# A hybrid encoder trunk on one core: the order of the branch weights' loads and of their split

## The reference, cut to what matters

```python
merged = None
for i, y_i in enumerate((ya, yb, yc)):
    z = cols(COL_Z + i * BRANCH_WIDTH, BRANCH_WIDTH)
    g = cols(COL_G + i * D_MODEL, D_MODEL)
    u = jax.nn.sigmoid(g) * ((y_i * jax.nn.silu(z)) @ w_br[i])
    merged = u if merged is None else merged + u
out = merged @ w_out
return x + gate[:, None, :] * out
```

## Time and profile before

| what | value |
|---|---|
| median of 3 runs | 2371.23 us (2370.74 to 2372.26) |
| time of the profiled execution | 2368.96 us |
| its span on the core | 2366.0 us |
| TensorE matmuls busy | 2309.8 us, 98% of the span |
| VectorE busy | 1624.0 us, 69% |
| ScalarE busy | 1123.7 us, 47% |
| DMA engines busy, all of SP's requests | 20.0% of 16 engines |
| granted TensorE clock, mean | 0.999 |

### The profile page before, as it was taken

The page is one execution under the profiler, slowest core; times in us unless marked ns, Lnnn a source line. Parts: engine busy times, 40 slices in busy tenths (PEclk is TensorE's granted clock), DMA queues, the critical chain, the costliest instruction groups (busy, mean ns, idle before and its releaser), DMA issues.

```text
span 2366.0 us, 41870 instructions
## 1 busy us (share of the span) xinstructions
PE 2309.8 (98%) x15466; PEld 2139.8 (90%) x15466; DVE 1624.0 (69%) x4481; ACT 1123.7 (47%) x3035; POOL 59.0 (2%) x103
## 2 busy tenths in 40 slices
PE   7999999999999999999999999999999999999999
PEld 5888888999999899999888889989999997999998
DVE  7877568577777575666578866775787765666772
ACT  5666457434444443334356674663444435333340
POOL 0010011000000000000001001100000000000000
PEclk9999999999999999999999999999999999999999
DMA  7221321121111322221521112112111122222223
GB/s 279 94 75 37 115 85 43 64 83 57 59 54 45 114 73 67 94 85 63 171 81 35 36 47 96 42 50 98 52 61 35 57 82 81 85 85 76 85 84 122
DMA packets 63034, 186.11 MB, mean 79 GB/s; under 512 B 9584, under 2 KB 22512, under 8 KB 59888
## 3 DMA queue, kind: packets, MB, share of 16 engines
q1 hardware_dynamic: 52320, 164.00, 20.0%
q10 hardware_dynamic: 10512, 19.44, 2.3%
HBM read 168.73 MB, written 12.58 MB: 77 GB/s over the span
## 4 chain that ended last, share of the span: by engine, by line
PE 85%; DVE 6%; ACT 4%; DMA 2%; issue 2%; SPq 0%; ACTq 0%; DVEq 0%
PE ps_proj L984 57%; PE ps_score L1028 7%; PE ps_pt L1028 6%; PE ps_score L1161 2%; PE ps_pt L1174 2%; PE ps_pv L1210 2%; PE ps_score L1145 1%; DMA wb_raw<-in_w_branch 1%; PE ps_tr L1225 1%; PE ps_pv L1191 1%; PE ps_tr L1226 1%; PE ps_pv L1204 1%; DMA w_raw<-in_w 1%; DVE w_lo L2311 1%; ACT act_hi L1435 1%
## 5 line engine op out<-in xcount | busy, mean ns | idle before, releaser
L984 PE MATMUL ps_proj<-w_hi,act_hi 128*128 128x384 f32 x1824 | 632.6, 347 | 3.3 <-ACT act_hi L1435 2.1
L984 PE MATMUL ps_proj<-w_hi,act_lo 128*128 128x384 f32 x1824 | 612.2, 336 | 0.0
L984 PE MATMUL ps_proj<-w_lo,act_hi 128*128 128x384 f32 x1824 | 611.8, 335 | 0.0
L984 PEld LDWEIGHTS ps_proj<-w_hi,act_hi 128*128 128x128 f32 x1824 | 342.8, 188 | 9.1 <-ACT act_hi L1435 5.8
L984 PEld LDWEIGHTS ps_proj<-w_lo,act_hi 128*128 128x128 f32 x1824 | 343.4, 188 | 0.0
L984 PEld LDWEIGHTS ps_proj<-w_hi,act_lo 128*128 128x128 f32 x1824 | 342.5, 188 | 0.0
L1954 DVE TENSOR_REDUCE ssq<-square 128x2 f32<-128x256 f32 (+1 forms) x228 | 95.6, 419 | 215.5 <-ACT square L1529 214.7
L1529 ACT ACTIVATE square<-ps_proj 128x256 f32<-128x256 f32 x228 | 88.2, 387 | 270.7 <-PE ps_proj L984 270.1
L2311 DVE TENSOR_TENSOR w_lo<-w_raw,w_hi 128x1536 fp32r<-128x1536 f32 (+3 forms) x121 | 188.7, 1560 | 12.6 <-ACT w_hi L1359 12.0
L1359 ACT ACTIVATE w_hi<-w_raw 128x1536 fp32r<-128x1536 f32 (+2 forms) x120 | 161.1, 1343 | 56.5 <-DMA w_raw<-in_w 33.0
L984 PE MATMUL ps_proj<-act_hi,w_hi 128*128 128x512 f32 (+1 forms) x512 | 174.4, 341 | 8.2 <-DVE w_lo L2311 4.8
(11 more groups left out here) (263 smaller groups left out, 4895.0 us busy)
## 6 DMA issues: line engine op xcount, KB each, us to landing
w_raw<-in_w SPq DMA_DIRECT2D x80, 768.0 KB, 5.2
w_raw<-in_w SPq DMA_DIRECT2D x40, 512.0 KB, 3.7
s_raw<-in_w_gate SPq DMA_DIRECT2D x72, 256.0 KB, 3.0
w_ada<-in_w_mod SPq DMA_DIRECT2D x11, 1536.0 KB, 6.7
wb_raw<-in_w_branch SPq DMA_DIRECT2D x24, 512.0 KB, 3.7
first_ada<-in_w_first SPq DMA_DIRECT2D x8, 1024.0 KB, 13.2
parked<-y_t ACTq DMA_DIRECT2D x4, 1536.0 KB, 7.1
w<-in_w_gate SPq DMA_DIRECT2D x24, 256.0 KB, 4.0
```

The lines of the kernel that those rows point to most:

```text
L984: op = pe.matmul(out, sta[s](k), mov[m](k), start=(k == 0 and n == 0), stop=(k == chunks - 1 and n == 2))
```

## The change

It has two parts.

In `load_groups`, the branch weights of group `g + 1` are asked for right behind the quarters of group `g`, and no longer at the head of group `g + 1`. Written out, the list of requests before was: branch(C0), branch(C1), quarters(C1), branch(C2), quarters(C2), ..., branch(A0), quarters(A0), back(A), branch(A1), quarters(A1), ... The list after is the same except around each `load_back`: ..., quarters(A0), branch(A1), back(A), quarters(A1), ..., and likewise for B. The waits of each request are what they were.

In the lists of ACT and DVE, in every group but the first of a layer and the last, `branch_high` moves from beside unit 1 to beside unit 2, and `branch_low` from beside unit 2 to beside unit 3. ACT's copy M1 (unit 2, for unit 1) then stands ahead of `branch_high`, and DVE's sum U2 (unit 3, for unit 2) ahead of `branch_low`.

```diff
@@ load_groups
                 for g in groups_of(l):
-                    load_branch(g)
                     if group_before(g):
                         load_quarters(g)
+                    else:
+                        load_branch(g)
+                    if not last_group(g):
+                        load_branch(group_after(g))
                     if g[2] == 0 and g[1] in PARKED:
                         load_back(l, g[1])
@@ scalar engine
                     if not last_group(g):
-                        if at == (1 if group_before(g) else 5):
+                        if at == (2 if group_before(g) else 5):
                             branch_high(group_after(g))
@@ vector engine
                     if not last_group(g):
-                        if at == (2 if group_before(g) else 6):
+                        if at == (3 if group_before(g) else 6):
                             branch_low(group_after(g))
```

## The result

The changed kernel takes 2356.71 us as the median of 6 runs (2353.22 to 2360.77), the kernel before 2371.73 us on the same chip (2369.96 to 2374.33). The ratio is 0.9938, with a 95% interval of 0.9928 to 0.9948: 15.0 us faster. The forecast was 2358.2, with a range of 2354.5 to 2363.0.

A forecast was written before the change was run, and what follows sets the result against it. TensorE, busy 98% of the span, was taken as the bound except for stalls in four merge groups. Their 2.86 + 3.92 + 4.08 + 2.16 = 13.0 us, off the 2371.23 median, gave 2358.2 us, range 2354.5 to 2363.0.

The forecast's parts named there:

- The place and the cause: Merge stage, four groups loading returned outputs: late branch weights delay U2 and product 4; 13.02 us lost, 8.85 of it idle.
- The landing: Branch weights requested ahead of returned outputs land 3.8 us after the request, at 947.3 in A0, where it was 951.5.
- Part 2, the order on ACT and DVE: M1 and U2 go before the splits: U2 at 6.43 us from group start, U3 done at about 954.7 in A0.
- What is late next: DVE's list behind U2 in A0: U3 1.0 us ahead of product 6, later steps within about 0.3 us of before.
- Ordinary groups: The 16 other merge groups where both splits move: TensorE stays full, price 0, length 22.88 us.
- The clock term: Clock lost behind the four idle times: 4.17 us, between 1.1 and 7.4, so a gain of 9.9 to 16.3.
- Rival 1: Request order doesn't set landing order; branch weights stay late, U3 waits: 2.4 us idle left, 2360.6 to 2363, chance 5%.
- Rivals 2 and 3: Four groups: wait moves to product 6, 2363 to 2365, 6%; or returned outputs become late, slower, 2376, 3%.

The follow-up runs named there:

- Part 1 alone: Changed kernel with the splits put back beside units 1 and 2, only the branch request staying ahead of the returned outputs: 2355.12 us against 2373.26, ratio 0.9926.
- part 2 alone: Kernel before with the splits beside units 2 and 3, the branch request staying behind the returned outputs: 2360.78 us, ratio 0.995.
- the split two later: Changed kernel with the splits one product later still, beside units 3 and 4: 2356.67 us, ratio 0.9932 to before.
- the returned outputs later: Changed kernel with returned outputs requested only after product 0 or product 2 of the group: 2354.32 us, ratio 0.992, or 2366.05 us, ratio 0.9968.
- the second trace of the changed kernel: Changed kernel run again, unedited: 2356.43 us, ratio 0.9929 to the kernel before.
- the second of before: Kernel before run again, unedited, for a second trace: 2373.32 us, ratio 1.0002.
- the last experiment: Changed kernel with returned outputs requested only after product 2 of the group, 6.4 us after its start: 2366.05 us, ratio 0.9968.

## Why the prediction was right, point by point

- **The place and the cause.** Right. The four groups were the only ones that changed between the traces, and the order of requests alone removed their excess. U2 was late because both splits of a late load stood ahead of it.
- **The landing.** I took 3.8 us with ends at 3.4 and 4.8. It came in at 3.5 to 4.3 in the four groups. The first returned half moved back by 0.7 us in A0, between the 0 and the 1.3 that I allowed. In B0 it moved back by more, 1.6 us: it is in 6.3 us after the group's start (1035.51 + 5.7 - 1034.90) where it was in after 4.7.
- **Part 2, the order on ACT and DVE.** Right to 0.1 us: U2 at 6.44 us from the group's start (949.81 - 943.37) for 6.43, U3's end at 954.65 for 954.7. But the sum counts both parts together, and part 2 brings nothing beside part 1. Part 1 alone gives all of the gain, part 2 alone some 12 us of it (2373.26 - 2360.78 = 12.5). The prediction says how each works and doesn't say that either would do; it is seen from its own numbers, since a landing at 947.3 puts the unmoved split's end at about 949.6, ahead of U2's 949.72.
- **What is late next.** U3 had 1.2 us in hand, where 1.0 was worked out. The step "stands within about 0.3 us of where it stood beside TensorE before" is right for the changed kernel: the read of the second branch product ended 0.88 us ahead of the fourth before and 0.76 after. But it hid that this is the tighter place.
- **Ordinary groups.** 0 predicted, 0 measured: 22.88 us before and after.
- **The clock term.** This is the mis-sized one. I took the 4.17 us of one execution; two further ones have 7.3 and 5.8 us beyond the idle time. The gain is so 13.0 us by the first trace and 15.0 to 16.8 by the medians, within the bound of 16.3 that I gave for it on one and above it by 0.5 on the other (interval of the second: 0.9917 to 0.9941, 14 to 20 us). The smallest remainder, 0.27 us, is not clock either: its groups are granted 1.00, and it is there behind each idle time, with a first matmul of 0.44 us for 0.33, so it goes with the restart of TensorE.
- **Rival 1.** Fell: the branch weights landed first because they were asked for first. The rule of the Trainium skill (DMA: Bandwidth & Descriptors, section Queues, rings and completion order), that completion is "not FIFO per issuing engine", says that the order is not assured. It doesn't say that a transfer asked for first lands with the later ones, so "by that rule this rival is what would happen" went too far. In A0 and B0 of all ten traces the branch weights landed ahead of both halves where they were asked for first, and behind both where they were asked for last. Its chain through U3, with the weights late, was seen in the later split alone, idle 2.23 us for 2.4, and cost 5.1 us and not 2.4, for the restarts and for DVE's late reads of the branch products.
- **Rivals 2 and 3.** Neither happened; the experiments with the split two later and the returned outputs later brought both about and found their points. DVE's list behind C12 may grow by about 0.8 us before TensorE is held up. `branch_low` may start 0.4 us later than that, since DVE is idle for 0.39 ahead of C12: 1.2 in all, where I had 1.4. The first half may land 9.2 us after the group's start, as forecast; in the changed kernel it lands at 949.0 - 943.4 = 5.6 in A0 and 6.3 in B0, so that 2.9 to 3.6 us are in hand where I had 2.9. The price that I gave beyond that point, 4 us for each us, left out restarts and the branch products: 1.7 us of lateness should have cost 6.8 and cost 9.6. With these figures the change becomes a loss at a landing of about 952.5 + (13.0 - 2.8) / 4 = 955.0 and not 955.8, an estimate.
- **Open.** The profiled span fell by only 8.8 us. From the last request ahead of it to C0, the stage before the merge of the second layer took 56.34 us after for 54.24 before, and the stretch below, granted 1.00 in the trace of before, was granted 0.94. No instruction was changed there and no wait is new. It belongs to that execution and not to the change: the second trace of the changed kernel has 54.02 us there, the second of before 54.45. The last stage tells the same, from the last branch request to the end: 119.4 us in this trace for 117.9 before and in the second trace of the changed kernel. These two stages are 3.6 of the 4.2 us that are missing. Why one execution loses clock in a place and another doesn't was not tried.

```profile
1958.00:1985.00 27.00, 24.67 (x208) 20.25 (x207) 10.76 (x33) 11.24 (x26) 0.00 (x0) 0.94 0.28 94
```

## What to carry to other kernels

When a wait in the chain is a load, look first at what was asked for ahead of it in the same queue: exchanging two requests that wait for the same event costs nothing if the one that moves back has measured room. On an engine that works its list strictly in order, put what TensorE waits for ahead of the preparation for later work, and then count every reader further down the list, down to the ones that free a bank. Size a stall from its idle time and its clock separately, and take the clock from more than one execution.

## What the runs showed of the hardware

In the four groups, idle times of TensorE of 1.9 to 3.6 us were followed by a drop from the 2.4 GHz to the 1.2 GHz level in some executions and not in others: two of four groups in one trace of before, four in another, three in a third. The idle time doesn't sort them. The 2.59 and 2.40 us were not followed by a drop, the 1.92 was. Nor did the loss grow with it: beyond the idle time the nine groups with a drop lost 1.73 to 1.87 us, for idle times of 1.92 to 3.57, and the three without one 0.27 to 0.28. In the output stage, behind idle times of 1.1 and 0.6 us, the stretch from 1130 to 1150 was granted 0.91 in five of the ten traces and 1.00 in the others. The idle times of 1.4 to 1.6 us in the last experiment came with a granted clock of 1.00 in its trace. The 512 KB of branch weights landed 3.4 to 4.3 us after their request ahead of the returned outputs, and 6.5 to 8.2 us behind them.
